# Attention in a fused two-layer kernel: query high and low parts turned together, block maxima turned as one and spread by a mask

## The reference, cut to what matters

```python
def block_attention(q, k, v):                 # blocks of 128 queries
    scale = HEAD_DIM ** -0.5                  # HEAD_DIM 64, 8 query heads, 2 key heads
    def one_block(qblk):
        s = jnp.einsum('bqkgd,bskd->bkgqs', qblk, k) * scale
        p = jax.nn.softmax(s, axis=-1)
        return jnp.einsum('bkgqs,bskd->bqkgd', p, v)
    ...
# q = rope(rmsnorm(q)), k = rope(rmsnorm(k)); latent queries attend to 1024 latent keys and
# 128 cached context keys in one softmax, context queries to 128 context keys
```

## Time and profile before

| | us |
|---|---|
| median of 3 runs | 1857.84 (1856.94 to 1862.08) |
| profiled execution | 1847.7 |
| its span | 1846.0 |
| TensorE matmul busy | 1678.0 (91%) |
| VectorE busy | 978.3 (53%) |
| GpSimd busy | 929.1 (50%) |
| ScalarE busy | 624.1 (34%) |

### The profile page before, as it was taken

The page is one execution under the profiler, slowest core; times in us unless marked ns, Lnnn a source line. Parts: engine busy times, 40 slices in busy tenths (PEclk is TensorE's granted clock), DMA queues, the critical chain, the costliest instruction groups (busy, mean ns, idle before and its releaser), DMA issues. The chain is left out here.

```text
span 1846.0 us, 40839 instructions
## 1 busy us (share of the span) xinstructions
PE 1678.0 (91%) x17404; PEld 1366.1 (74%) x17404; DVE 978.3 (53%) x1476; ACT 624.1 (34%) x1238; POOL 929.1 (50%) x858
## 2 busy tenths in 40 slices
PE   4999999989988899979849999999899888999798
PEld 3898999979975455548628989998799754455586
DVE  2646316367746785561126462163777467955611
ACT  4322310144442444451143222111444424444511
POOL 1003395089944878833210034940899448788332
PEclk8999999999998999989969999999999989999899
DMA  9301113110000020022283011131000000200222
GB/s 336 120 14 59 61 58 94 58 37 21 5 12 13 6 63 12 12 115 91 91 315 124 14 59 61 58 99 59 31 22 4 12 13 6 64 12 12 115 91 91
DMA packets 71246, 117.22 MB, mean 64 GB/s; under 512 B 10128, under 2 KB 42128, under 8 KB 71056
## 3 DMA queue, kind: packets, MB, share of 16 engines
q1 hardware_dynamic: 70128, 114.18, 18.3%
q10 hardware_dynamic: 928, 0.34, 0.1%
HBM read 95.03 MB, written 19.47 MB: 62 GB/s over the span
## 5 line engine op out<-in xcount | busy, mean ns | idle before, releaser
L1407 POOL TENSOR_TENSOR attn_accp<-attn_accp,attn_pr 128x1024 f32<-128x1024 f32 x112 | 268.8, 2400 | 49.2 <-ACT attn_pr L1473 43.3
L93 PE MATMUL ps<-h_hi,in_w_hi 128*128 128x384 f32 (+1 forms) x816 | 275.8, 338 | 5.0 <-DVE h_lo L456 4.9
L94 PE MATMUL ps<-h_lo,in_w_hi 128*128 128x384 f32 (+1 forms) x816 | 274.6, 336 | 0.0
L95 PE MATMUL ps<-h_hi,in_w_lo 128*128 128x384 f32 (+1 forms) x816 | 274.5, 336 | 0.0
L1660 DVE TENSOR_REDUCE attn_ql<-ps 128x1 f32<-128x1152 f32 x128 | 173.0, 1355 | 121.8 <-PE ps L1587 121.5
L1473 ACT ACTIVATE attn_pr<-ps 128x512 f32<-128x512 f32 x292 | 158.7, 595 | 189.9 <-PE ps L1624 189.0
L93 PEld LDWEIGHTS ps<-h_hi,in_w_hi 128*128 128x128 f32 (+1 forms) x816 | 150.0, 184 | 13.2 <-issue 6.7
L95 PEld LDWEIGHTS ps<-h_hi,in_w_lo 128*128 128x128 f32 (+1 forms) x816 | 150.0, 184 | 3.9
L94 PEld LDWEIGHTS ps<-h_lo,in_w_hi 128*128 128x128 f32 (+1 forms) x816 | 150.0, 184 | 3.9
L1623 PEld LDWEIGHTS ps<-attn_QH,attn_KH 128*128 128x128 f32 x292 | 55.4, 190 | 126.4 <-issue 53.5
L1633 PE MATMUL ps<-attn_pr,z 128*64 128x512 f32 x520 | 141.3, 622 | 0.0
(11 more groups left out here) (248 smaller groups left out, 3604.2 us busy)
## 6 DMA issues: line engine op xcount, KB each, us to landing
in_w<-in_w_in SPq DMA_DIRECT2D x22, 1024.0 KB, 6.1
zz<-in_w_mod SPq DMA_DIRECT2D x8, 2048.0 KB, 13.6
gates<-in_gate SPq DMA_DIRECT2D x48, 192.0 KB, 1.9
attn_gt<-gates SPq DMA_DIRECT2D x34, 256.0 KB, 2.6
z<-in_w_mod SPq DMA_DIRECT2D x4, 2048.0 KB, 10.1
out_w<-in_w_out SPq DMA_DIRECT2D x16, 512.0 KB, 6.6
delta_GB<-gc_rows SPq DMA_DIRECT2D x36, 128.0 KB, 3.0
z<-out_y SPq DMA_DIRECT2D x9, 512.0 KB, 10.5
```

Source lines behind the costliest of these rows:

```text
L93: nc.tensor.matmul(out, a_hi(i), b_hi(i), start=(i == 0), stop=False)
L94: nc.tensor.matmul(out, a_hi(i), b_lo(i), start=False, stop=False)
L95: last = nc.tensor.matmul(out, a_lo(i), b_hi(i), start=False, stop=(i == n - 1))
L1407: nc.gpsimd.tensor_tensor(acc, a, pr[:, n % 4], ALU.add).then_inc(pool_added, 1)
```

## The change

High and low parts of a query block now stand side by side (qhl), and one turn of four transposes gives both: partitions 0 to 63 hold qh, 64 to 127 ql. ScalarE copies all of it to QH, and partitions 0 to 63 a second time to QM. The keys' parts change places in khl, so that KH now holds kh twice and KO holds kl. The first product gives kh·qh + kh·ql, the second kl·qh − max. The products for the maxima use QH and KH as before.

The four maxima of an item are four columns of a small tile mx. One transpose of 128x4 puts them in partitions 0 to 3 of bank 7, and VectorE multiplies them, repeated four times, with a 4x4 unit mask into partitions 64 to 67 of QM: row r holds the maxima of block r in its own 128 columns and zero elsewhere. KO has four rows of −1 there. This lo item is now VectorE's work; it stands in VectorE's queue at lo's rank. In the scan, each key turn is copied out by three ScalarE instructions of 64 partitions (KH twice, KO once) before it counts as copied, and `keys_copied` is gone. `query_high` writes once instead of twice, and `split` casts once.

```diff
-    QL, rc = sb("QL", [P, 2, 2, QB], F32R), sb("rc", [P, 2, QB])
+    rc = sb("rc", [P, 2, QB])
...
-    QH = sb("QH", [P, 3, 2, QB], F32R)
-    qhh, ql = sb("qhh", [P, 4, 4, P]), sb("ql", [P, 4, 4, HD + 2])
+    QH, QM = sb("QH", [P, 3, 2, QB], F32R), sb("QM", [P, 3, 2, QB], F32R)
+    qhl, mx = sb("qhl", [P, 4, 4, P]), sb("mx", [P, 4, 4])
...
-            for e in range(2 if n >= 4 else 0):
-                nc.gpsimd.tensor_copy(blocks(qhh[:, n % 4, :, HD * e:HD * e + HD], p).bitcast(F32R), q)
+            hi, lo = (blocks(qhl[:, n % 4, :, HD * e:HD * e + HD], p) for e in range(2))
             if n >= 4:
+                nc.gpsimd.tensor_copy(hi.bitcast(F32R), q)
                 pool.drain()
-            nc.gpsimd.tensor_tensor(blocks(ql[:, n % 4, :, 0:HD], p), q, blocks(qhh[:, n % 4, :, 0:HD], p),
-                                    ALU.subtract).then_inc(q_split, 1)
+            nc.gpsimd.tensor_tensor(lo, q, hi, ALU.subtract).then_inc(q_split, 1)
...
-                copied(item, query_columns(QH[:, p % 3], p, i), turned_columns(slice(0, P), p))
-            elif item[0] == "lo":
-                _, p, i = item
-                r = slice(0, HD + 1)
-                copied(item, query_columns(QL[r, p % 2], p, i), turned_columns(r, p))
+                is_turned(act, *item)
+                nc.scalar.activation(query_columns(QH[:, p % 3], p, i), turned_columns(slice(0, P), p), ACT.Copy)
+                nc.scalar.activation(query_columns(QM[0:HD, p % 3], p, i), turned_columns(slice(0, HD), p),
+                                     ACT.Copy).then_inc(turn_copied, 1)
...
-            nc.scalar.activation(KH[:, :, 256 * j:256 * j + 256], ps[:, K_BANKS[j], :].rearrange("p (g c) -> p g c", g=2),
-                                 ACT.Copy).then_inc(k_act, 1)
+            lo, hi = (ps[HD * e:HD * e + HD, K_BANKS[j], :].rearrange("p (g c) -> p g c", g=2) for e in range(2))
+            cols = slice(256 * j, 256 * j + 256)
+            nc.scalar.activation(KH[HD:P, :, cols], hi, ACT.Copy)
+            nc.scalar.activation(KH[0:HD, :, cols], hi, ACT.Copy)
+            nc.scalar.activation(KO[0:HD, :, cols], lo, ACT.Copy).then_inc(k_act, 1)
...
-                for blk in range(4):
-                    last = nc.tensor.transpose(ps[0:HD + 1, 7, P * blk:P * blk + P], ql[:, n % 4, blk, 0:HD + 1], m["ident"])
-                last.then_inc(turned, 1)
+                nc.tensor.transpose(ps[0:4, 7, 0:P], mx[:, n % 4, :], m["ident"]).then_inc(turned, 1)
...
-                nc.tensor.matmul(ps[:, e, :], KO[0:HD + 1, g, ks], QL[0:HD + 1, p % 2, e, :],
+                nc.tensor.matmul(ps[:, e, :], KO[0:HD + 4, g, ks], QM[0:HD + 4, p % 3, e, :],
...
+            elif item[0] == "lo":                      # VectorE
+                _, p, i = item
+                is_turned(dve, *item)
+                rows = slice(HD, HD + 4)
...
+                    out = QM[rows, p % 3, :, 256 * i:256 * i + 256].rearrange("p h (t c) -> p h t c", c=P)
+                    shape = [4, 2, 2, P]
+                    row = ps[0:4, 7, 0:P].unsqueeze(1).unsqueeze(1)
+                    own = m["ident"][0:4, 0:4].rearrange("p (h t) -> p h t", t=2).unsqueeze(3)
+                nc.vector.tensor_tensor(out, row.broadcast_to(shape), own.broadcast_to(shape), ALU.mult).then_inc(turn_copied, 1)
```

More of the change, by code:

```diff
@@ L1267, in attention @@
     pr, gt, accp = sb("pr", [P, 4, 2, QB]), sb("gt", [P, 2, QB]), sb("accp", [P, 2, 2, QB])
-    QL, rc = sb("QL", [P, 2, 2, QB], F32R), sb("rc", [P, 2, QB])
+    rc = sb("rc", [P, 2, QB])
     osq, oss = sb("osq", [P, NT, 256]), sb("oss", [P, NT, 4])
+    sb("gap", [P, 1408])
     KH, KO = sb("KH", [P, NKV, N_KEYS], F32R), sb("KO", [P, NKV, N_KEYS], F32R)
@@ L1411, in key_low @@
             for ks, k in keys_of(j):
-                last = nc.gpsimd.tensor_tensor(khl[:, ks, :, HD:P], k, khl[:, ks, :, 0:HD], ALU.subtract)
+                last = nc.gpsimd.tensor_tensor(khl[:, ks, :, 0:HD], k, khl[:, ks, :, HD:P], ALU.subtract)
             last.then_inc(k_split, 1)
@@ L1423, in gpsimd @@
         pool.drain()
[L1424 removed]
+        nc.gpsimd.memset(KO[HD:HD + 4].bitcast(F32), -1.0).then_inc(ones_done, 1)
         pool.drain()
@@ L1478, in key_high @@
             for ks, k in keys_of(j):
-                last = nc.scalar.activation(khl[:, ks, :, 0:HD].bitcast(F32R), k, ACT.Copy)
+                last = nc.scalar.activation(khl[:, ks, :, HD:P].bitcast(F32R), k, ACT.Copy)
             last.then_inc(k_high, 1)
@@ L1483, in query_high @@
             n = ASKS.index((p, i))
-            for e in range(2):
-                last = nc.scalar.activation(blocks(qhh[:, n % 4, :, HD * e:HD * e + HD], p).bitcast(F32R), queries(p, i), ACT.Copy)
-            last.then_inc(q_high, 1)
+            nc.scalar.activation(blocks(qhl[:, n % 4, :, 0:HD], p).bitcast(F32R), queries(p, i), ACT.Copy).then_inc(q_high, 1)
         def keys_turned(j):
             act.wait_ge(k_turned, j + 1)
-            nc.scalar.activation(KH[:, :, 256 * j:256 * j + 256], ps[:, K_BANKS[j], :].rearrange("p (g c) -> p g c", g=2),
-                                 ACT.Copy).then_inc(k_act, 1)
[L1493 to L1496, removed]
+            lo, hi = (ps[HD * e:HD * e + HD, K_BANKS[j], :].rearrange("p (g c) -> p g c", g=2) for e in range(2))
[3 more added lines that the diff above has]
+            nc.scalar.activation(KO[0:HD, :, cols], lo, ACT.Copy).then_inc(k_act, 1)
         for j in range(4):
@@ L1511, in scalar @@
         evict(("hi", 0, 1))
-        for j in range(3):
-            keys_copied(j)
         evict(("hi", 1, 0))
-        for j in range(3, 5):
-            keys_copied(j)
         act.wait_ge(on_in, 32)
@@ L1539, in query_turn @@
         for blk in range(4):
-            last = nc.tensor.transpose(ps[:, 7, P * blk:P * blk + P], qhh[:, n % 4, blk, :], m["ident"])
+            last = nc.tensor.transpose(ps[:, 7, P * blk:P * blk + P], qhl[:, n % 4, blk, :], m["ident"])
         last.then_inc(turned, 1)
@@ L1656, in maximum @@
             if p == 0:
-                nc.vector.tensor_reduce(ql[:, a % 4, :, HD], ps[:, bank, :].rearrange("p (h c) -> p h c", c=P), AX_X,
+                nc.vector.tensor_reduce(mx[:, a % 4, :], ps[:, bank, :].rearrange("p (h c) -> p h c", c=P), AX_X,
                                         ALU.max).then_inc(mx_read, 1)
             else:
-                nc.vector.tensor_reduce(ql[:, a % 4, blk, HD:HD + 1], ps[:, bank:bank + 3, 0:GRP], AX_XY,
+                nc.vector.tensor_reduce(mx[:, a % 4, blk:blk + 1], ps[:, bank:bank + 3, 0:GRP], AX_XY,
                                         ALU.max).then_inc(mx_read, 1)
@@ L1665, in work @@
                 maximum(*item[1:])
+            elif item[0] == "lo":
+                _, p, i = item
+                is_turned(dve, *item)
+                rows = slice(HD, HD + 4)
+                if p == 0:
+                    out, shape = QM[rows, 0, i, :].rearrange("p (b c) -> p b c", c=P), [4, 4, P]
+                    row, own = ps[0:4, 7, 0:P].unsqueeze(1), m["ident"][0:4, 0:4].unsqueeze(2)
+                else:
+                    out = QM[rows, p % 3, :, 256 * i:256 * i + 256].rearrange("p h (t c) -> p h t c", c=P)
[3 more added lines that the diff above has]
+                nc.vector.tensor_tensor(out, row.broadcast_to(shape), own.broadcast_to(shape), ALU.mult).then_inc(turn_copied, 1)
             elif item[0] == "recip":
```

5 lines of the change are left out of this document (2 added, 3 removed).

## The result

The changed kernel took 1916.86 us in the median of 4 runs (1912.24 to 1920.83), the kernel before 1857.39 us (four runs; the table ahead of the prediction has three of them): a ratio of 1.0327, with a 95% interval of 1.0305 to 1.035. It is slower, as forecast, but by 59.5 us where 41.0 were forecast, and 2.9 us beyond the upper end of the range. The profiled execution's span is 1910.6 us, 64.6 us over that of before.

The account below looks back on a forecast made before the run. TensorE, busy 91% of the span, was taken to bound the kernel. Terms of 17.7 us a layer, 35.4 for two, plus 5.6 for the clock made 41.0, so 1857.8 became 1898.8 us; range 1876 to 1914.

Parts of the forecast that it names:

- What bounds the kernel, and the mechanism: TensorE bounds; VectorE's spread queues behind the reduction, so TensorE waits 1.35 us after slots 17, 35, 44, 53: +5.3 us a layer.
- The price of the spread: VectorE's spread takes 0.68 us, like the normalisation of line 1678, without contending with GpSimd.
- Slots 13, 11 and 16, and the second copy elsewhere: O turn waits for the spread in 13, +2.4 us; for ScalarE's second copy in 11 and 16, +1.1; elsewhere hidden.
- Slot 8: The o turn waits for the spread behind oscale on VectorE, starting at 614.1 instead of 609.91: +4.2 us a layer.
- Slots 22 to 31: Late spread in slot 26 costs +5.1 us, old waits in 27 to 30 partly vanish: net +2.1 us to slot 32.
- The scan: ScalarE's extra key copies delay the last key turn 2.5 us and the first query turn another 0.4: +2.9 us a layer.
- Ahead of slot 0: Three spreads between VectorE's last reductions, then hi(2, 0)'s longer copying before the first exponentials: together +1.3 us a layer.
- The clock: TensorE's clock falls to half after slots 8 and 26 in each layer, four falls at 1.4 us: +5.6 us.
- The clock that holds: Rival: the waits come but TensorE's clock doesn't fall, 1893.2 us; chance 0.17.
- the dear spread: Rival: the spread takes 1.30 us, ten times a layer on the path, 12.4 us more: 1911 us; chance 0.10.
- the half case: Rival: key copies and slots 8 and 26 hide better, half of the sum stays: 1876 us; chance 0.10.
- the sides without a loss: Rivals: the spread costs nobody anything, 1847.5 us, chance 0.09; or gains and waits cancel within 0.3%, chance 0.04.

Follow-up runs that it names:

- e1: Changed kernel with lo's rank set to -1, so VectorE's spread comes ahead of the slot's reduction: 1874.75 us, ratio 1.0105 to the kernel before.
- e3: Changed kernel with the turn's bank freed after the first of ScalarE's two copies of a hi item, the second reading SBUF: 1921.39 us, ratio 1.0364.
- e6: e1 with the first exponentials put ahead of the copies of hi(2, 0) in ScalarE's queue: 1872.93 us, ratio 1.0098 to the kernel before.
- e7: e1 with matrix products that nobody reads put between TensorE's work ahead of slot 0: 1869.00 us, ratio 1.008 to the kernel before.
- e4: Changed kernel with VectorE's spread done a second time, into an unused tile, ahead of each: 1939.15 us, ratio 1.0453 to the kernel before.
- e5: Changed kernel with all repairs (spread first, two copies per key turn, bank freed early, exponentials first, lo(2, 1) and last keys' parts earlier): 1851.14 us, ratio 0.9969.

## Why the prediction was right or wrong

**What bounds the kernel, and the mechanism: right.** TensorE waits for a spread that VectorE does behind its reduction. Slots 35, 44 and 53 grew by 1.44 us where 1.35 were forecast, slot 17 by 1.48. e1 changes the queue's order alone, and of the 21.7 us that the slots of a layer had lost, 1.4 to 3.0 are left.

**The price of the spread: right.** 0.682 us for 36 of them, for 0.68 from the normalisation's row; every one of them took 0.681 to 0.683 us, whether it ran wholly beside a GpSimd instruction (757.83) or beside none (582.45). The Trainium skill (SBUF — State Buffer, Who interferes with whom) says that a VectorE instruction with at most one SBUF input, outside the modes that use both ports, doesn't contend with GpSimd; the trace agrees, with these 0.68 us. The changed kernel's groups by line:

```profile
L1611 PE MATMUL ps<-attn_QH,attn_KH 128*128 128x512 f32 x292 | 138.1, 473 | 26.4 <-DVE attn_QM L1666 22.8 <-ACT attn_pr L1472 3.6
...
L1666 DVE TENSOR_TENSOR attn_QM<-ps,masks 4x512 fp32r<-4x512 f32 x36 | 24.5, 682 | 3.4 <-PE ps L1559 2.4
...
L1456 ACT ACTIVATE attn_QM<-ps 64x512 fp32r<-64x512 f32 x36 | 21.0, 582 | 0.0
...
L1595 PE MATMUL ps<-masks,of 128*128 128x128 f32 x36 | 8.4, 321 | 23.6 <-DVE attn_QM L1666 17.5 <-ACT attn_QM L1456 4.8 <-ACT attn_rc L1449 1.4
```

The scores now sit idle for 22.8 us and the o turns for 17.5 us on attn_QM's spread; neither row had such a releaser before:

```profile
L1623 PE MATMUL ps<-attn_QH,attn_KH 128*128 128x512 f32 x292 | 131.8, 451 | 2.5 <-ACT attn_pr L1473 2.5
...
L1606 PE MATMUL ps<-masks,of 128*128 128x128 f32 x36 | 7.4, 288 | 7.0 <-ACT attn_QH L1449 2.9 <-ACT attn_QL L1449 2.7 <-ACT attn_rc L1449 1.4
```

**The shorter turn: right.** Seven slots a layer are 0.31 to 0.34 us shorter, for 0.32.

**Slots 13, 11 and 16, and the second copy elsewhere: right.** +2.5 for 2.4, and +0.5 twice for 1.1 in all; the copy is free in the others, as e3 shows from the other side.

**Slot 8: the wait right, the clock left out.** +5.4 for 4.2. The o turn starts 7.09 us into the slot (619.90, 626.99), for 2.87 before: 4.2 us later, as counted. The rest is that the o turn and the weighted values behind it already ran at half clock (0.69 us for 0.44, 1.98 for 1.08). The forecast sign of scores waiting in slot 9 didn't show, since the o turn ahead of them had waited already.

**Slots 22 to 31: right within a microsecond, in part by luck.** +2.9 us, for 2.1 and a fall of the clock at 1.4. The wait in slot 26 was shorter than counted (+4.3 for 5.1), slot 27 at half clock took 1.7 us more, and slot 24 grew by 0.3 (as did 33, beyond this stretch), which nothing in the prediction had. That slots 28 to 30 give back 2.7 us of old waits is the give-back that was worked out.

**The scan: place right, size short.** +3.4 us to the last key turn for 2.5: the copies start 0.60 to 0.61 us apart, where 0.55 was taken, and twelve precede that turn. Then +1.1 for 0.4, and +1.2 us to the square for nothing: the table of stretches has 7 us at half clock in the scan, where the kernel before had none. In all 5.7 us a layer for 2.9. The key turn's own wait, 3.96 us, is the 4 us that the prediction named as a sign.

**Ahead of slot 0: size short.** +2.8 us a layer for 1.3. The three spreads between the reductions cost 1.0, near the 0.75 that was counted for them after the shorter turns. The step to slot 0 grew by 1.8 where 0.55 was counted; it is ScalarE's queue and half clock together (e6, e7).

**The clock: this is the step that failed.** The prediction named the mechanism, and priced a fall at 1.4 us, which holds (slots 14 and 18, which hold no wait of their own, grew by 1.5 and 1.4, and slot 18 lost it again in e4, where the clock held). It counted two falls a layer, 5.6 us for both layers, and let the rival be that there are none. There are seven stretches: in the scan, two ahead of slot 0 that run into slot 0, and after slots 8, 13, 17 and 26, in all 51.5 us at half clock for 13.6 before, so 38 us more a layer. What they cost in sum isn't measured apart, since the waits that cause them go with them. Summed from the parts that grew beyond the queue's count, it is 1.2 (slot 8), 1.3 (slot 9), 1.5 (14), 1.4 (18), 1.5 (slots 0 and 1), 0.8 in slots 22 to 31, about 1.3 ahead of slot 0 and about 1.9 in the scan, some 11 us a layer for 2.8: an estimate, and 16 of the 18.5 us that the forecast fell short. That slots 8, 14 and 18 are long by the clock is seen in their instructions or in e4; that all the rest of this sum is the clock's is argued, the scan's 1.9 us above all. I had looked for falls only behind the two longest idle times, and not where the change thins TensorE's work by adding steps on VectorE and ScalarE between its own, as ahead of slot 0.

A further 3.9 us of the profiled span lie ahead of the keys' high part, where nothing was changed; e1's profile had 1.0 us less than the kernel before there in layer 0. In its layer 1, the stretch from slot 71 to the keys' high part took 4.3 us more. I take the 3.9 us for scatter.

**The rivals.** The clock that holds (it fell behind 1.71 us idle in slot 17), and the dear spread, are both refuted; so are the half case and the sides without a loss. e5 shows from what point the latter would have come true: with the spread ahead of the reduction and the copies off the path.

## What to carry to other kernels

An operation moved to an idle engine costs its place in that engine's queue, not its duration: 0.68 us of work cost 1.4 us in the plain slots and 4.2 us, 5.4 with the fallen clock, where that engine was behind. When a value is awaited by the engine that sets the pace, put its producer first in its slot, before long work that nobody awaits; here one number in a rank table was worth 42 of the 59.5 us. And count the clock for each place where the pace-setting engine's work is thinned, not only behind its longest wait.

## What the runs showed of the hardware

ScalarE's copies don't all overlap alike: a 128x512 copy and the 64x512 copy behind it start 0.49 us apart (587.91, 588.40), three 64x512 copies of which the first writes partitions 64 to 127 start 0.60 us apart (542.42, 543.02, 543.62), each 0.58 to 0.60 us long. What makes the difference is not settled here. A spread that writes 4 partitions takes as long (0.682 us) as an instruction on 128 (0.684).

The clock doesn't follow the length of a wait alone. In the changed kernel TensorE is idle for the same 1.71 us behind slots 17, 35, 44 and 53, and the clock fell behind slot 17 only, in both layers. In e4_spread_twice it is idle for 2.31 us behind each of the four, and in both layers the clock fell behind slots 35 and 53 and held behind slots 17 and 44. So a wait of 1.7 to 2.3 us can go either way, and a forecast should carry both.
